# GpSimd takes over one low part of an expert weight during the routing of a hybrid decoder layer

## The reference

```
g_logits = (h @ w_rg).astype(jnp.float32) + b_rg
grp = jnp.argmax(g_logits, axis=-1)                 # one of 4 groups
e_in = ...                                          # the 8 expert logits of that group
top_p, top_e = lax.top_k(jax.nn.softmax(e_in, axis=-1), 2)
gate = p_grp[:, None] * top_p / jnp.sum(top_p, axis=-1, keepdims=True)
...                                                 # assignments sorted by expert, padded to blocks of 128
def expert_block(args):
    xi, e = args
    gu = xi @ w_up[e]                               # 1024 x 1024
    g, u = jnp.split(gu, 2, axis=-1)
    return (jax.nn.silu(g) * u) @ w_down[e]         # 512 x 1024
```

## Time and profile before

| | us |
|---|---|
| median of 3 runs | 1762.59 (1761.45 to 1764.46) |
| profiled execution, its own time | 1762.01 |
| its span in the trace | 1760.4 |
| TensorE matmul busy | 1688.4 |
| VectorE busy | 1284.0 |
| ScalarE busy | 886.8 |
| GpSimd busy | 355.0 |
| routing (first VectorE step to first expert product) | 1127.17 to 1154.39 |

### The profile page before, as it was taken

How to read it: one execution, slowest core, us unless ns; L and a number is a source line. 1 busy time by engine, 2 the same in 40 slices (tenths; PEclk the granted TensorE clock), 3 DMA queues, 4 the chain that set the end, 5 groups by cost and what they waited for, 6 DMA issues and landing times. The chain is left out here.

```text
span 1760.4 us, 25342 instructions
## 1 busy us (share of the span) xinstructions
PE 1688.4 (96%) x8669; PEld 1401.0 (80%) x8671; DVE 1284.0 (73%) x1687; ACT 886.8 (50%) x1123; POOL 355.0 (20%) x293
## 2 busy tenths in 40 slices
PE   7999999999999998999999999689999999999996
PEld 5887888787888887899987788578888888887774
DVE  4024888699999907877658853488888888888884
ACT  6115652211111115678751111478778777777774
POOL 3111122332222210011000000174222221222221
PEclk9999999999999999999999999899999999999998
DMA  5325233422222337446508645489999999999993
GB/s 195 100 97 159 108 116 147 157 101 96 96 96 96 115 101 169 102 120 137 144 22 267 202 156 202 194 297 384 362 369 354 366 355 350 360 353 350 369 365 88
DMA packets 110225, 361.71 MB, mean 205 GB/s; under 512 B 18379, under 2 KB 22475, under 8 KB 110144
## 3 DMA queue, kind: packets, MB, share of 16 engines
q1 hardware_dynamic: 96644, 339.38, 55.9%
q0 software_dynamic: 13504, 21.28, 4.8%
HBM read 315.51 MB, written 62.91 MB: 215 GB/s over the span
## 5 line engine op out<-in xcount | busy, mean ns | idle before, releaser
L1832 DVE TENSOR_TENSOR ex_wl<-ex_raw,ex_wh 128x2048 fp32r<-128x2048 f32 x192 | 437.6, 2290 | 78.9 <-ACT ex_wh L1828 78.5
L1828 ACT ACTIVATE ex_wh<-ex_raw 128x2048 fp32r<-128x2048 f32 x192 | 367.5, 1916 | 107.9 <-DMA ex_raw<-in_w_expert_up 50.2
L83 PE MATMUL gs_banks<-hT_hi,gs_wh 128*128 128x512 f32 x512 | 199.8, 390 | 2.6 <-POOL gs_wl L769 1.4
L84 PE MATMUL gs_banks<-hT_lo,gs_wh 128*128 128x512 f32 x512 | 199.2, 389 | 0.0
L85 PE MATMUL gs_banks<-hT_hi,gs_wl 128*128 128x512 f32 x512 | 199.2, 389 | 0.0
L825 ACT ACTIVATE gs_wh<-gs_raw 128x1024 fp32r<-128x1024 f32 x30 | 31.8, 1061 | 253.2 <-PE gs_banks L85 253.2
L889 DVE MATCH_REPLACE8 selm<-sg_top,selm 128x512 f32<-128x512 f32 (+5 forms) x160 | 139.0, 877 | 0.0
L885 DVE MAX8 sg_top<-selm 128x8 f32<-128x512 f32 (+5 forms) x160 | 134.2, 881 | 0.0
L1682 PE MATMUL at_ops<-at_v,at_pT 128*128 128x65 f32 (+1 forms) x984 | 125.0, 269 | 0.0
L769 POOL TENSOR_TENSOR gs_wl<-gs_raw,gs_wh 128x1024 fp32r<-128x1024 f32 x30 | 73.0, 2435 | 238.8 <-ACT gs_wh L825 238.8
L1682 PEld LDWEIGHTS at_ops<-at_v,at_pT 128*128 128x128 f32 x984 | 120.0, 192 | 0.9
(11 more groups left out here) (363 smaller groups left out, 3682.7 us busy)
## 6 DMA issues: line engine op xcount, KB each, us to landing
ex_raw<-in_w_expert_up SPq DMA_DIRECT2D x128, 1024.0 KB, 21.2
ex_raw<-in_w_expert_down SPq DMA_DIRECT2D x64, 1024.0 KB, 21.3
gs_raw<-in_w_gate SPq DMA_DIRECT2D x32, 512.0 KB, 3.5
gatesT<-sg_go SPq DMA_DIRECT2D x32, 512.0 KB, 2.6
selm<-gatesT SPq DMA_DIRECT2D x32, 512.0 KB, 4.4
at_qk<-qkh SPq DMA_DIRECT2D x52, 256.0 KB
at_qk<-qkl SPq DMA_DIRECT2D x44, 256.0 KB
gs_raw<-in_w_qk SPq DMA_DIRECT2D x17, 512.0 KB, 4.8
```

Of the source, the lines that this page charges most:

```text
L83: pe.matmul(out, a_hi, b_hi, start=(k == 0), stop=False)
L84: pe.matmul(out, a_hi, b_lo, start=False, stop=False)
L1828: act.activation(ring.wh[r][:, :, :], ring.raw[slot][:, :, :], ACT.Copy).then_inc(ring.w_high, 1)
L1832: dve.tensor_tensor(ring.wl[r][:, :, :], ring.raw[slot][:, :, :], ring.wh[r][:, :, :].bitcast(F32), ALU.subtract).then_inc(ring.w_low, 1)
```

## The change

The low part of pair 2 is made by GpSimd, between its clearing of `xg` and `gather_found(0)`, after the waits for the high part of that pair and for the starting count of `w_low`. VectorE no longer makes it and waits for it ahead of `x_lo(0, 0)`. Its other low parts stay where they were.

```diff
-            low_in_route(IN_ROUTE[0])
+            dve.wait_ge(ring.w_low, IN_ROUTE[0] + 1)
             x_lo(0, 0)
             for p in IN_ROUTE[1:]:
                 low_in_route(p)
...
+            pool.wait_ge(ring.w_high, IN_ROUTE[0] + 1)
+            pool.wait_ge(ring.w_low, IN_ROUTE[0])
+            split_low(pool, ring, IN_ROUTE[0], IN_ROUTE[0] % RING)
             pool.wait_ge(cleared, 2)
             for stored in landed:
                 for s in range(2):
```

## The result

The changed kernel takes 1771.51 us on the median of 7 runs (1767.85 to 1773.73), the kernel before, with its further runs, 1764.46 on the median of 7. The ratio is 1.0040, 95% interval 1.0027 to 1.0054: slower, by some 7 us. It was measured three more times on other chips, and the ratio was 1.0055, 1.0051 and 1.0047.

The account below looks back on a forecast made before the run. Bound: an expert stage fed by unbroken transfers, so its start, set by the routing chain, counts. Removed work and GpSimd's gain count 0, the held routing step 4.2 us: 1762.6 becomes 1766.8 us, range 1763.6 to 1769.2.

Parts of the forecast that it names:

- VectorE's part is not on the path: Ahead of x_lo: removing VectorE's 2.28 us subtraction gains 0, since x_lo waits for ScalarE; VectorE idles 3.92 us instead.
- GpSimd's subtraction holds a routing step to its end: In the routing: GpSimd's subtraction keeps VectorE's step L2018 out until it ends, making all later steps 4.2 us late.
- bounds 3.94 to 4.68: Range of the routing step's delay, from a 4.52 us subtraction let in early to a 4.82 us one let in late.
- the 4.67 of the line: Length of GpSimd's 2048-column subtraction, 4.67 us, from a line through the medians at 512 and 1024 columns.
- the estimate of 3.9 us: The routing step's delay if GpSimd's subtraction takes the skill page's 4497 ns and enters behind L2016: 3.9 us.
- the same wrong point of entry: In the routing: GpSimd gets in at 1131.90, behind L2016, so L2018 of 1132.19 is the step held.
- The open question: Routing steps have 64 columns; no row showed one kept out: full delay by the lock rule, 0 if only long steps are.
- The clock against the shift: Turning of the first rows: TensorE's clock rise against the shift could change its 1.45 us by at most 0.7 us.
- The shift goes through to the end: Expert stage: first product and transfers shift together, so the 4.2 us delay still stands at the last product.
- Gained on GpSimd: ... Value: 0: GpSimd's first note gets some 1.6 us shorter, but that is lost waiting before the gather at 1168.53: value 0.
- The rivals: Four alternatives: not slower (0.10), delay partly given back in the expert stage (0.08), more than the sum (0.08), faster (0.02).
- The third: Rival in the routing: longer subtraction, late entry or late clock rise; two more microseconds give 1768.8 us; chance 0.08.

Follow-up runs that it names:

- e9: The kernel before, with VectorE's low part of pair 3 ahead of x_lo instead of behind it, first measurement: 1761.23 us, ratio 0.9992.
- e14: The kernel before, with VectorE's low part of pair 3 ahead of x_lo, measured a second time: 1761.43 us, ratio 0.9998.
- e8: The changed kernel, with GpSimd's subtraction moved behind its second gather: 1768.29 us, ratio 1.0039.
- the half run: The changed kernel, but GpSimd subtracts only the first 1024 columns and VectorE the others at the old place: 1767.48 us, ratio 1.0016.
- e1: The changed kernel again, unaltered, on another chip for a second trace: median 1772.98 us, its profiled execution 1768.51 us.
- e3: The kernel before, VectorE's part kept, plus a GpSimd subtraction of 128x2048 at the place of the change, result overwritten: 1769.91 us, ratio 1.0034.
- e6: The kernel before, with two overwritten VectorE subtractions of 2048 columns added in the routing, nothing added on GpSimd: 1768.74 us, ratio 1.0038.
- e7: The changed kernel, with GpSimd's first four notes held back until the first rows are turned: 1767.15 us, ratio 1.0028.
- e10: The changed kernel, with VectorE's low part of pair 3 moved ahead of x_lo: 1766.56 us, ratio 1.0018.
- e11: Against the kernel before, VectorE makes pair 2's low part in the routing plus one overwritten subtraction; no GpSimd subtraction: 1771.23 us, ratio 1.0051.
- e13: The changed kernel, with a GpSimd memset in place of its subtraction, second run: 1766.61 us, ratio 1.0026.
- e2: The changed kernel, with a GpSimd memset in place of its subtraction, first run: 1765.40 us, ratio 1.0007.

## Why the prediction was wrong

**VectorE's part is not on the path.** Right. VectorE was idle ahead of x_lo in every trace but those of e9 and e14, where the part added there filled the wait, and these two runs changed nothing that can be measured.

**GpSimd's subtraction holds a routing step to its end.** Right in kind and nearly in size: 4.57 us (4.79 - 0.22) against 4.2, bounds 3.94 to 4.68. The subtraction took 4.52, the lower bound, not the 4.67 of the line. The figure of 4497 ns in the Trainium skill ("GPSIMD Engine Reference", "Performance versus the Vector engine") was nearer to that length; the estimate of 3.9 us made from it was farther off, because it used the same wrong point of entry. The held step was L2015 and not L2018, and it began at 1132.68, 0.19 ahead of GpSimd's recorded start (0.66 ahead in e8): a step whose row begins just ahead of GpSimd's can be held as well. The open question, whether 64 columns are kept out, is answered: they are, in this case's traces. That agrees with the rule of the Trainium skill ("SBUF — State Buffer", "SBUF: two separate sides") that the shared ports are locked for a whole instruction. Twice the columns, from the half run to the full one, made the hold about twice as long (2.41, 4.57).

**The clock against the shift.** Put at up to 0.7 either way; it gave back 0.5 (e1: 4.14 late at the first product with 4.57 held).

**The shift goes through to the end.** Right within what the traces can tell: over all 17 traces it is 602.9 to 611.9 us from the first product to the end, before 606.0, with no order by shift. The four runs with the whole shift and no late signal in their trace (e3, e6, e7, e10) are 1.0034, 1.0038, 1.0028 and 1.0018, 3.2 to 6.7 us, on average 5.2; their first products come 4.0 to 4.5 us late. 4.1 us (1.0023) lies in three of the intervals and just under the lower end of the fourth, 1.0025. The 1 us between is not explained.

**"Gained on GpSimd: ... Value: 0".** This is the step that failed. I saw that VectorE's subtraction had kept the first note waiting for 1.6 us and counted the end of that as a gain without value. It was a cover. With the notes free to go out while TensorE sums the gates and turns the rows, TensorE's signal comes about 4 us late in 3 of 4 traces of the changed kernel, which in those doubles what the held step cost: 8.15 to 8.37 us instead of 4.1 at the first product. The times agree: the four measurements of the changed kernel are on average 8.5 us over before, 3.3 more than the runs with the shift alone, and 4.25 us in three of four executions would be 3.2. Shown for it: the late signal comes and goes with the notes' place, without the subtraction on GpSimd (e11), without a later routing (e13), and not when the notes are held (e7) or covered (e3, e6, e10).

**The rivals.** None of the four had this mechanism. The third, "more than the sum", had the direction, with causes that did not occur: the subtraction was not longer and was not let in late, and the clock's rise was not late for the turning. The fall of the clock behind the late signal is real (0.50 for some 7 us), but the stage behind the first product is not longer for it: 606.7, 606.1 and 607.7 us with it, 608.0 in e1 without.

What stays open is how free notes delay TensorE's signals. The profile has TensorE's turning at its normal place and names no engine as the one that released those who waited; and one pair of equal kernels, e2 and e13, shows it once and not the other time.

## What to carry to other kernels

Work moved to an engine that looks idle has to be laid against what its port shares: one GpSimd operation that reads SBUF held a 64-column VectorE step to its end, and in a chain of dependent steps its whole length is the price. And work that is taken away may have been holding something else back: ask what was queued behind it and what will now run earlier, beside whom, before that is booked as a gain. Where the executions of a kernel fall into groups, one trace shows only one of them. And when an engine that waits starts late though the work that it waited for is recorded on time, look at when the signals before that one came.

## What the runs showed that I had not expected

- The late signal: x_hi 3.7 to 4.2 us behind its place in 6 of 8 traces with free notes, and in those TensorE's signal for the sums of gates late before it.
- A VectorE cast of 16 columns from fp32 to bf16, with one input, was held for 5.0 us (5.22 against 0.18) by the subtraction, whose row begins 0.66 us later (e8).
- GpSimd's memset of 2048 columns (1.82 us) held none of the steps beside it.
- The held step's row began 0.19 us ahead of GpSimd's, and it was held all the same.
